# Two MLPs on one core: hidden tiles loaded from the scalar queue, weights staged further ahead, two banks for first and last products, first operands reordered

## The reference, cut to what matters

```python
def modulate(h, shift, scale):
    return h * (1.0 + scale[:, None, :]) + shift[:, None, :]
def sq_relu_mlp(h, w1, w2):
    return jnp.square(jax.nn.relu(h @ w1)) @ w2       # w1: 1024 x 4096, w2: 4096 x 1024

for i in range(DEPTH):                                # DEPTH = 2
    mod = c_act @ ada_w[i] + ada_b[i]                 # ada_w[i]: 1024 x 6144
    sh1, sc1, g1, sh2, sc2, g2 = jnp.split(mod, 6, axis=-1)
    h = modulate(rmsnorm(x, norm_mix_g[i]), sh1, sc1)
    ...                                               # pool mixer (i = 0), gated mixer (i = 1)
    x = x + g1[:, None, :] * y
    h = modulate(rmsnorm(x, norm_mlp_g[i]), sh2, sc2)
    x = x + g2[:, None, :] * sq_relu_mlp(h, mlp_w1[i], mlp_w2[i])
```

## Time and profile before

| | |
|---|---|
| runs | 2794.09, 2795.22, 2798.67 us |
| profiled execution | 2795.24 us |
| its span (first to last instruction) | 2793.4 us |
| mean granted TensorE clock | 0.959 |
| PE busy | 2536.5 us (91%) |
| DVE, ACT, POOL busy | 57%, 35%, 18% |
| mean traffic | 142 GB/s |

### The profile page before, as it was taken

The page is one execution under the profiler, slowest core; times in us unless marked ns, Lnnn a source line. Parts: engine busy times, 40 slices in busy tenths (PEclk is TensorE's granted clock), DMA queues, the critical chain, the costliest instruction groups (busy, mean ns, idle before and its releaser), DMA issues.

```text
span 2793.4 us, 32220 instructions
## 1 busy us (share of the span) xinstructions
PE 2536.5 (91%) x11664; PEld 2041.4 (73%) x11664; DVE 1587.5 (57%) x2414; ACT 986.8 (35%) x1622; POOL 507.1 (18%) x427
## 2 busy tenths in 40 slices
PE   8979998777777899999799979999999999999998
PEld 3657777666666778887577767777788888787677
DVE  5865465465555653435555545555555121999873
ACT  2346564100000132233456540000133112888861
POOL 1342321000000020014323200000001000457741
PEclk9989999988898999999899999999999999999999
DMA  7624445544444372033244463333323446334621
GB/s 276 241 76 151 165 175 197 207 160 151 151 166 151 121 229 69 1 121 106 103 154 158 158 256 121 136 136 136 106 106 121 136 146 166 85 91 132 176 89 61
DMA packets 219076, 396.87 MB, mean 142 GB/s; under 512 B 59441, under 2 KB 136369, under 8 KB 218929
## 3 DMA queue, kind: packets, MB, share of 16 engines
q1 hardware_dynamic: 218928, 394.93, 42.0%
HBM read 285.83 MB, written 115.08 MB: 144 GB/s over the span
## 4 chain that ended last, share of the span: by engine, by line
PE 68%; DMA 11%; DVE 10%; issue 4%; ACT 3%; POOL 3%; SPq 1%; DVEq 0%; POOLq 0%; ACTq 0%
PE banks L2304 18%; PE banks L2305 17%; PE banks L2306 17%; DMA stage<-w 5%; DMA stage<-ada_w 4%; PE banks L2816 2%; PE banks L2834 2%; PE banks L2394 2%; ACT Whi L1262 1%; DVE Hlo L1879 1%; DVE acc L1701 1%; DMA hidden<-first_slot 1%; PE banks L2602 1%; PE banks L2601 1%; PE banks L2603 1%
## 5 line engine op out<-in xcount | busy, mean ns | idle before, releaser
L2304 PE MATMUL banks<-MB,Whi 128*128 128x512 f32 x1024 | 419.4, 410 | 137.0 <-DVE X L1998 133.7
L2304 PE MATMUL banks<-Hhi,Whi 128*128 128x512 f32 x1248 | 495.5, 397 | 6.4 <-DVE Wlo L1723 3.3
L1998 DVE SCALAR_TENSOR_TENSOR X<-banks,mod,X 128x512 f32<-128x512 f32 x512 | 374.2, 748 | 216.4 <-PE banks L2306 214.6
L2305 PE MATMUL banks<-Hlo,Whi 128*128 128x512 f32 x1248 | 487.6, 391 | 0.0
L2306 PE MATMUL banks<-Hhi,Wlo 128*128 128x512 f32 x1248 | 486.9, 390 | 0.0
L2305 PE MATMUL banks<-MB,Whi 128*128 128x512 f32 x1024 | 412.3, 403 | 0.0
L2306 PE MATMUL banks<-MB,Wlo 128*128 128x512 f32 x1024 | 411.2, 402 | 0.0
L1262 ACT ACTIVATE Whi<-stage 128x2048 fp32r<-128x2048 f32 x59 | 112.8, 1912 | 797.3 <-DMA stage<-w 759.1
L2304 PEld LDWEIGHTS banks<-MB,Whi 128*128 128x128 f32 x1024 | 201.2, 196 | 191.5 <-DVE X L1998 98.5
L2304 PEld LDWEIGHTS banks<-Hhi,Whi 128*128 128x128 f32 x1248 | 235.6, 189 | 65.4 <-DVE Hlo L1879 6.5
L2305 PEld LDWEIGHTS banks<-Hlo,Whi 128*128 128x128 f32 x1248 | 235.6, 189 | 49.9 <-issue 2.4
(11 more groups left out here) (243 smaller groups left out, 4046.9 us busy)
## 6 DMA issues: line engine op xcount, KB each, us to landing
stage<-w SPq DMA_DIRECT2D x64, 1024.0 KB, 7.3
MB<-hidden SPq DMA_DIRECT2D x64, 1024.0 KB, 5.4
hidden<-slot SPq DMA_DIRECT2D x112, 512.0 KB, 2.6
stage<-ada_w SPq DMA_DIRECT2D x48, 1024.0 KB, 7.5
x_saved<-X SPq DMA_DIRECT2D x32, 512.0 KB, 2.7
stage<-w_in SPq DMA_DIRECT2D x13, 1024.0 KB, 6.2
X<-x_saved SPq DMA_DIRECT2D x24, 512.0 KB, 6.1
hidden<-first_slot SPq DMA_DIRECT2D x16, 512.0 KB, 2.6
```

The lines of the kernel that those rows point to most:

```text
L1998: nc.vector.scalar_tensor_tensor(out=X[:, k, half(hf)], in0=Dn[:, i % D_BANKS, :], scalar=gate[:, k:k + 1], in1=X[:, k, half(hf)], op0=ALU ...
L2304: nc.tensor.matmul(out_bank, whi, xhi, start=start, stop=False, skip_group_check=onto)
L2305: nc.tensor.matmul(out_bank, whi, xlo, start=False, stop=False, skip_group_check=onto)
```

## The change

1. **Down.** The hidden tiles of chunk c + 2 are loaded by DMAs that ACT issues, not SP. All later units (w2, ada_w, the unit behind the MLP) are loaded by `fetch` from one list, `stream`, up to three (pairs) or three and the current one (down) ahead of their use. SP has no other wait in down.
2. **ada_w.** Three of the modulations' totals are made between the pairs (12 passes, pairs 1 to 12, in X row 2), four in down (16 passes; two in chunks 1 and 2, one in 3 to 14).
3. **Pairs.** Bank D is 0 for even and 5 for odd pairs, and PE's waits for joins move to the product that uses the bank. Chunk 0 of down waits for the last two joins only at tiles 2 and 3.
4. **Start.** `combine`, `first_tile` and `ops` are interleaved. Tiles 4 to 7 are emptied inside pairs 0 to 3, into places of their own (`later_full`, `later_slot`), T1's sums wait for all of the norm.

```diff
-    def fast_bank(name):
+    def fast_bank(name, g):
-        return PS_ALL[:, {"A": 1, "B": 3, "C": 4, "D": 0}[name], :]
+        return PS_ALL[:, {"A": 1, "B": 3, "C": 4, "D": (0, 5)[g % 2]}[name], :]
+    def first_places(i):
+        full, slot = (first_full, first_slot) if i < 4 else (later_full, later_slot)
+        return full[:, i % 2, :], slot
+    def hidden_tiles(c, hf):
+        return MB[:, c % 2, :, hf, :].bitcast(F32), hidden[2 * c:2 * c + 2, hf].rearrange("f p n -> p f n")
...
     def ada_total(l, cc):
-        return X[:, 2, :] if (l, cc) == (0, 5) else acc[:]
+        return X[:, 2, :] if (l, cc) in ((0, 5), (1, 0), (1, 1)) else acc[:]
...
-        def mlp(l, with_ada):
+        def mlp(l, with_ada, after, then):
             split(src_in(w1[l], 1))
-            stream = [(src_in(w1[l], c + 2), c) for c in range(PAIRS)] + [(src_w2(l, 0), PAIRS)]
             if with_ada:
-                for q in range(4):
-                    at = 10 + 2 * q
-                    stream.insert(at, (src_ada(0, 5, q), None))
+                early = {p: ((0, 5), (1, 0), (1, 1))[(p - 1) // 4] + ((p - 1) % 4,) for p in range(1, 13)}
+                passes = iter((1, cc, q) for cc in range(2, 6) for q in range(4))
+                late = {c: [next(passes) for _ in range(2 if c < 3 else 1)] for c in range(1, CHUNKS - 1)}
+            stream = [src_in(w1[l], 2)]
+            for p in range(PAIRS):
+                if p in early:
+                    stream.append(src_ada(*early[p]))
+                stream.append(src_in(w1[l], p + 3) if p < PAIRS - 1 else src_w2(l, 0))
+            for c in range(CHUNKS - 1):
+                stream += [src_ada(*a) for a in late.get(c, ())] + [src_w2(l, c + 1)]
+            stream.append(after)
...
-            def fetch():
+            def fetch(depth):
-                if fetched < len(stream):
+                while fetched < min(consumed + depth, len(stream)):
...
-            do["combine"](T, l, 0, base)
             do["first_up"](T, l, 0)
-            T.add(c=1, a=4)
-            do["combine"](T, l, 1, base)
-            do["ops"](T, base, range(4), None)
+            T.add(c=1)
             do["first_up"](T, l, 1)
-            do["ops"](T, base, range(4, 7), None)
+            do["combine"](T, l, "S")
+            do["combine"](T, l, "T1")
+            do["first_tile"](T, l, 0)
+            do["combine"](T, l, "T3")
+            do["first_tile"](T, l, 1)
+            do["ops"](T, base, (0, 1))
+            do["first_tile"](T, l, 2)
+            do["combine"](T, l, "T2")
+            do["ops"](T, base, (2, 3))
+            do["first_tile"](T, l, 3)
+            do["ops"](T, base, (4,))
+            do["combine"](T, l, "T4")
+            do["ops"](T, base, (5, 6))
             used()
             for p in range(PAIRS):
-                fetch()
-                while stream[consumed][1] is None:
-                    ...
+                fetch(3)
+                if p in early:
+                    if p > 1 and early[p][2] == 0:
+                        mods(*early[p - 1][:2])
+                    ada_ahead(*early[p])
+                    fetch(3)
+                elif p - 1 in early:
+                    mods(*early[p - 1][:2])
                 do["fast"](T, l, p, base, unit, p == PAIRS - 1)
...
-            for c in range(CHUNKS - 1):
-                if with_ada and 2 <= c < 14:
-                    for n in range(2):
-                        ada(1, (c - 2) // 2, 2 * (c % 2) + n)
-                step("down", src_w2(l, c + 1), D16, mod[:, l, 5 * KT:6 * KT], l, c)
-                if with_ada and 2 <= c < 14 and c % 2 == 1:
-                    mods(1, (c - 2) // 2)
+            for c in range(CHUNKS):
+                for a in late.get(c, ()):
+                    fetch(4)
+                    ada_ahead(*a)
+                fetch(4)
+                do["fetched_split"](T, None)
+                used(w=1)
+                do["down"](T, gate, l, c, then if c == CHUNKS - 1 else None)
+                if c in late and late[c][-1][2] == 3:
+                    mods(*late[c][-1][:2])
...
@@ SP: down() with its hidden loads is gone; ACT, in down():
+                if c == 0:
+                    for b, _, _ in BLOCKS:
+                        act.wait_ge(m_stored[b], 16 * T.n["f"])
+                if c + 2 < CHUNKS:
+                    for hf in range(NH):
+                        act.wait_ge(d_ready, T("d", KT * (hf + 1)))
+                        nc.scalar.dma_start(*hidden_tiles(c + 2, hf)).then_inc(m_loaded[c % 2][hf], 16)
...
@@ POOL, in right_sum():
                 if name == "T1":
-                    pool.wait_ge(tb_ready, T("b", KT + k + 1 - 2 * KT))
-                    pool.wait_ge(lo_done, T("h", k + 1 - 2 * KT))
+                    pool.wait_ge(lo_done, T("h"))
...
@@ ACT, in fast():
-                    act.wait_ge(f_stored, 16 * 8 * (l + 1))
...
                 after(2)
+                if p < 4:
+                    first_tile(T, l, 4 + p)
                 after(3)
@@ PE, in mods():
+                reach(pe, a_free, T("a"))
@@ PE, in fast():
                     if q == 0:
-                        pe.wait_ge(a_free, T("a"))
-                        reach(pe, joined, 5 * g)
+                        pe.wait_ge(a_free, T("a", -4 if p == 0 else -3))
+                        reach(pe, joined, 5 * g - 5)
...
+                    if q == 3:
+                        reach(pe, joined, 5 * g - 1)
@@ PE, in down():
-                if c == 0:
-                    pe.wait_ge(joined, 5 * T.n["f"])
+                if c == 1:
                     pe.wait_ge(m_relu, 4 * T.n["f"])
...
+                        if c == 0 and i in (2, 3):
+                            pe.wait_ge(joined, 5 * T.n["f"] + i - 3)
```

More of the change, by code:

```diff
@@ L632, in mlp @@
                 used()
-                unit = T.n["u"]
             T.add(w=1)
@@ L685, in walk @@
         norm(3, "project")
-        mlp(1, False)
-        step("down", src_in(w_in2, 0), D16, mod[:, 1, 5 * KT:6 * KT], 1, CHUNKS - 1, 4)
+        mlp(1, False, src_in(w_in2, 0), 4)
         do["spill"](T)
@@ L1398, in first_up, with combine @@
[L1398 to L1410 removed]
+            def combine(T, l, name):
+                for k in range(KH2 if name in SUMS else 0):
+                    n = 16 * l + KH2 * SUMS.index(name) + k
+                    act.wait_ge(sums_made, n + 1)
+                    if name == "T1" and k == 0:
+                        act.wait_ge(gap_ready, l + 1)
+                    if name == "T4" and k == 0:
+                        act.wait_ge(a_ready, T("a"))
+                    nc.scalar.activation(right_side(name, k)[0], sum_place(name, k), ACT.Identity,
+                                         bias=sum_shift(l, name, k)).then_inc(sums_hi, 1)
@@ new lines, in first_tile @@
+            def first_tile(T, l, i):
+                n = 8 * l + i
+                full, slot = first_places(i)
+                act.wait_ge(a_ready, T("a", i + 1 - 8))
+                reach(act, f_lo, n - 1)
+                nc.scalar.activation(full, first_bank(i), ACT.Relu).then_inc(a_free, 1)
+                act.wait_ge(a_free, T("a", i + 1 - 8))
+                nc.scalar.activation(full, full, ACT.Square).then_inc(f_square, 1)
+                act.wait_ge(f_square, n + 1)
+                reach(act, f_stored, 16 * n)
+                nc.scalar.activation(slot[:, 0, :], full, ACT.Copy).then_inc(f_hi, 1)
@@ L1943, in join @@
                 dve.wait_ge(product_done, 7 * g + product + 1)
-                nc.vector.tensor_tensor(out, fast_bank(bank), other, ALU.add).then_inc(joined, 1)
+                nc.vector.tensor_tensor(out, fast_bank(bank, g), other, ALU.add).then_inc(joined, 1)
             def hidden_lo(g, n):
```

164 lines of the change are left out of this document (65 added, 99 removed).

## The result

The changed kernel takes 2567.77 us (median of 4 runs, 2565.11 to 2568.83) against 2794.66 us, a ratio of 0.9184 with an interval of 0.9168 to 0.92. The forecast of 2545 was 22.8 us low and its range of 2530 to 2585 holds the time. The profiled execution took 2567.97 us, of which 2566.2 is the span, 227.2 us shorter than the span before.

A forecast was written before the change was run, and what follows sets the result against it. TensorE was taken as the bound, busy 91% of the span, its largest wait at the down matmuls. Savings of 136.1 + 36.7 + 17.2 + 15.5 + 23.0 + 21.4 = 249.9 from 2795.24 gave 2545 us, range 2530 to 2585.

The forecast's parts named there:

- Part 1: Down: hidden loads on ACT's queue and weights three units ahead give 21.76 us chunks; saves 136.1 and 36.7 us.
- Rival B: First down stage: the transfers are the limit, not their order; 62 us less saved, 2607; chance 0.06.
- Rivals C: Down: the stage ring does not run ahead, loads still leave near the chunk's begin; 76 us less saved, 2621; chance 0.06.
- D: Down: a DMA issue holds ACT; slower than before from 15.4 us an issue, 2923 at 20 us; chance 0.01.
- Double passes: First MLP's down: two chunks with two ada_w passes cost 1.3 us each, 2.6 in all.
- I take 2.0 us: Chunk 0 of down: wait for the late reload of X's row 7, 2.0 us (0 to 8).
- Part 2: Pairs 1 to 13: alternating bank D turns 20.17 us a pair into 19.04; saves 17.2 and 15.5 us.
- about 1.6: First MLP's pairs: PE's wait in us at each of three modulations, with 1.7 of matmuls 3.3 each.
- with about 1 us to spare: Pairs 1 to 3: the first tile's added work on ACT and DVE stays covered before the sixth product.
- Part 3: Start of each MLP: reordered operands cut the first product's wait from 18.9 to 0.9 us; saves 23.0 and 21.4.
- 1.0 (0 to 4): Pair 0: us of waiting because the join before the sixth product may be late, ACT being behind.
- Rival A: Start of each MLP stays long, one late step in ACT's reordered queue holding all; +24 us, 2569; chance 0.14.

The follow-up runs named there:

- run 2: run 1 with the weights in the down stages fetched one unit deep instead of four; 2697.36 us.
- run 1: Changed kernel with the hidden loads of down issued by SP again instead of ACT, same waits; 2568.54 us.
- run 8: Changed kernel with SP's two hidden loads for the second down chunk behind the reload of X's row 7; 2558.55 us.
- run 4: Changed kernel with bank D the same one in every pair, so product 0 waits for the last join of the pair before; 2591.60 us.
- run 7: Changed kernel with the modulation products waiting for DVE's ada pass alone, not for the following pair's last operand; 2559.12 us.
- run 9: Changed kernel with the edits of run 5, run 7 and run 8, plus DVE's first_tile in pairs 0 to 3 behind joins 1 and 2; 2534.73 us.
- run 5: Changed kernel with POOL's T1 sums waiting tile by tile instead of for the whole norm; 2558.25 us.
- run 3: run 1 with the weights in the down stages fetched two units deep instead of four; 2595.28 us in one run.
- run 6: Changed kernel with ACT's bank A copy and DVE's joins first in pair 0, and DVE's first tile behind the joins in pairs 1 to 3; 2554.05 us.

## Why the prediction was right, and where it was off

- **Part 1, the mechanism.** Right: weights and ada units that stand behind SP's wait are what made the chunks long, and run 2 brings 128 of the 164 us of both stages back by that alone. The forecast took two measures together, the wait out of SP's queue and the units further ahead. With the second, the first adds nothing (run 1); whether the first is enough by itself, as the code says, was not run. Rival B (transfers as the limit) falls, the first down stage now moves 194 GB/s. Rivals C and D fall with chunks of 21.76 us.
- **Part 1, its sizes.** Double passes 2.7 us against 2.6, modulations 1.70 each against 1.7. The step that failed is "I take 2.0 us" for chunk 0: 6.5 and 5.85 us (within its 0 to 8). I saw that SP waits for a store and gave that store 4 to 6 us to land, but let row 3 go out in time; it, too, stands behind a store. The two stores took 7.1 and 7.4 us in L0, behind two large hidden loads on full engines (0.92; run 8). Those loads stood there in the kernel before too, where rows 3 and 4 left 1.4 us into chunk 0 (493.82) and the wait for the weights hid it. That is 4.5 and 3.85 us of the error; what is left in L0 is 0.5.
- **Part 2.** Bank D exact in L1 (247.5 against 247.52; run 4). In L0 it is 6.9 us off in three steps. "about 1.6" for the modulation's wait was 2.26 once and 1.4 twice; the pairs with it are 23.27, 22.45 and 22.45 us, 1.1 more in all than priced. I put no price on the clock after it: 1.7 us in each of two following pairs (0.14 of it stays without slow matmuls, run 7), though I had written that idle time takes slow matmuls with it. And "with about 1 us to spare" for tiles in pairs 1 to 3 held in L1, which has no passes over ada_w; in L0 pairs 2 and 3 lost 0.8 and 1.4 us (run 9 mends both).
- **Part 3.** The largest error, 7.6 and 8.35 us. The wait at the first product was 1.53 and 2.35 us against 0.9, in its bounds. What failed is "1.0 (0 to 4)" inside pair 0: it was 26.9 us, 7.9 above dense, beyond my bound. The 12 sums were timed well (21.61 / 12 = 1.80 us against 1.88), but I followed their lateness only to the first product. They also push T4's lower parts, the last operand and so POOL's first sum for the next pair, and ACT's copy for the fifth product stands behind that. With the sums tile by tile the start is 19.98 and 19.94 us (run 5), so 20.9 was a fair price for the new order without that one wait, and the changed wait was the mis-sized term. Behind the two waits of about 2 us the matmuls that start 0.43 us apart make up 3.4 us of the 7.9 (17 of them at 0.2 us each).
- **Outside the terms.** The same wait gave 3.1 us back ahead of the start in L0, as DVE's steps at the norm's end no longer stand beside POOL, and 4.9 of the 6.25 in L1 (run 5). The forecast had named the later start and only its cost. So the total looks better than its terms: they are 31.7 us short, and 9.0 us that nobody had priced hide a part.
- **Rival A** described this (10 to 12 us in each MLP and 2569 in all). Its time is 1.2 us from the result, its mechanism partly so: the stall was a step that waits for POOL, not one that waits for a store, and in pair 0, not before it. I gave it 0.14.

## What to carry over

In a queue that issues in order, look at what stands behind each wait: fetches that stood ahead of it instead of behind it were worth 129 us, and once they did, a second queue for the wait brought nothing more. When a stage is reordered, follow the late step through the whole first iteration, every engine's next instruction included, and price a stall like these (1.45 us and more) with the slow matmuls that may follow it. When the largest wait goes, the next one behind it shows, as the late rows of X did: put the small transfers that someone waits for ahead of the large ones that nobody needs yet.

## What the runs showed of the hardware

- PE idle for 0.88 us ahead of each pair left the granted clock at 1.00 (run 4). Idle times of 1.45 to 2.3 us at the modulations, each followed by some 2 us of narrow products, had 7 to 12 matmuls 0.43 us apart behind them in some places (pairs 4 and 8 of the changed kernel, 4 and 12 of run 3) and none in others (12, and 8 in run 3). Inside pair 0 of the changed kernel 2.21 us were followed by at least 7, inside pair 1 of run 6 2.87 us by none. Of two equal waits one costs 1.7 us more; what decides it is open.
- Two stores of 512 KB behind large loads took 7.1 and 7.4 us to land (issued at 460.70 and 468.62, the reloads that wait for them at 467.79 and 476.07), where the median of the 112 stores of this kind is 2.6 us.
- DVE's 128x512 step with two inputs in SBUF took 0.74 us alone and 1.12 beside POOL's sums; the lower parts of T took 1.77 us at 147.87, about one POOL sum (1.80).
